# Seven products per pair: three of them take high and low token parts as one operand, and the order of the work around them

## What is computed

```python
def swiglu(x, w_gu, w_down):
    a, b = jnp.split(x @ w_gu, 2, axis=-1)
    return (jax.nn.silu(a) * b) @ w_down

for i in range(DEPTH):          # DEPTH = 2
    x = layer_norm(ALPHA * x + 0.5 * swiglu(x, ffn1_w_gu[i], ffn1_w_down[i]), ...)
    y, qm = gla_mix(x @ gla_w_in[j], ...)      # layer 0; conv_mix in layer 1
    m = mem_attention(qm, mem, mem_w_kv[i])
    x = layer_norm(ALPHA * x + jnp.concatenate([y, m], axis=-1) @ w_out, ...)
    x = layer_norm(ALPHA * x + 0.5 * swiglu(x, ffn2_w_gu[i], ffn2_w_down[i]), ...)
```

## Time and profile before

| | |
|---|---|
| median of three runs | 2028.52 us (2028.18 to 2030.37) |
| the profiled execution's own time | 2027.72 us |
| its span | 2025.7 us |
| granted clock of TensorE, mean | 0.998 |
| TensorE | 2007.7 us busy, 99% |
| VectorE | 1355.1 us, 67% |
| ScalarE | 811.9 us, 40% |
| GpSimd | 816.3 us, 40% |

### The profile page before, as it was taken

How to read it: one execution, slowest core, us unless ns; L and a number is a source line. 1 busy time by engine, 2 the same in 40 slices (tenths; PEclk the granted TensorE clock), 3 DMA queues, 4 the chain that set the end, 5 groups by cost and what they waited for, 6 DMA issues and landing times.

```text
span 2025.7 us, 33884 instructions
## 1 busy us (share of the span) xinstructions
PE 2007.7 (99%) x13253; PEld 1839.4 (91%) x13253; DVE 1355.1 (67%) x1851; ACT 811.9 (40%) x1165; POOL 816.3 (40%) x575
## 2 busy tenths in 40 slices
PE   9999999999999999999999999999999999999998
PEld 9899998888988999999899999989887799999887
DVE  4477774554425768887466888746899986777646
ACT  5433351263433354444234444423353434434422
POOL 1588830044423357880015877001100435887000
PEclk9999999999999999999999999999999999999999
DMA  7533332332212235453232545323544222332222
GB/s 253 208 125 124 124 130 91 113 102 67 84 32 73 96 103 164 147 166 107 92 103 94 166 145 166 107 95 101 187 125 177 83 97 92 104 104 93 86 96 99
DMA packets 227015, 239.10 MB, mean 118 GB/s; under 512 B 5935, under 2 KB 219309, under 8 KB 225132
## 3 DMA queue, kind: packets, MB, share of 16 engines
q1 hardware_dynamic: 225196, 234.63, 35.2%
q10 hardware_dynamic: 1728, 3.21, 0.5%
HBM read 215.80 MB, written 22.02 MB: 117 GB/s over the span
## 4 chain that ended last, share of the span: by engine, by line
PE 89%; DVE 4%; POOL 3%; ACT 2%; issue 2%; DMA 1%; DVEq 0%; SPq 0%; ACTq 0%; POOLq 0%
PE bank L1879 12%; PE bank L1881 12%; PE bank L1880 12%; PE bank L2015 11%; PE bank L2017 11%; PE bank L2016 11%; PE bank L1890 3%; PE bank L1891 3%; PE bank L1892 3%; PE bank L1969 1%; ACT whi L712 1%; DVE wlo L1191 1%; PE bank L1974 1%; PE bank L2339 1%; PE bank L2338 1%
## 5 line engine op out<-in xcount | busy, mean ns | idle before, releaser
L712 ACT CAST whi<-raw 128x2048 fp32r<-128x2048 f32 (+3 forms) x190 | 322.8, 1699 | 866.2 <-POOL scratch L596 435.0
L1191 DVE TENSOR_TENSOR wlo<-raw,whi 128x2048 fp32r<-128x2048 f32 (+2 forms) x164 | 360.9, 2200 | 232.9 <-ACT whi L712 232.7
L573 POOL TENSOR_TENSOR tiny<-tiny 128x2 f32<-128x2 f32 (+1 forms) x13 | 9.4, 726 | 567.1 <-DVE tiny L1471 567.1
L536 POOL TENSOR_TENSOR wlo<-raw,whi 128x256 fp32r<-128x256 f32 x128 | 101.5, 829 | 300.4 <-DVE wlo L1191 176.2
L592 POOL TENSOR_TENSOR raw<-raw 128x512 f32<-128x512 f32 x72 | 217.2, 3017 | 0.0
L1879 PE MATMUL bank<-h_hi,whi 128*128 128x512 f32 x528 | 207.1, 392 | 0.0
L1881 PE MATMUL bank<-h_hi,wlo 128*128 128x512 f32 x528 | 205.5, 389 | 0.0
L1880 PE MATMUL bank<-h_lo,whi 128*128 128x512 f32 x528 | 205.5, 389 | 0.0
L596 POOL TENSOR_TENSOR scratch<-raw,s 128x512 f32<-128x512 f32 x72 | 152.9, 2124 | 53.7 <-DVE ex_lo L1198 53.7
L2015 PE MATMUL bank<-t_hi,ex_hi 128*128 128x256 f32 x576 | 164.0, 285 | 1.5 <-DVE bank L1250 0.9
L2015 PE MATMUL bank<-t_hi,whi 128*128 128x256 f32 x576 | 163.7, 284 | 1.7 <-DVE bank L1258 1.7
(11 more groups left out here) (376 smaller groups left out, 5807.9 us busy)
## 6 DMA issues: line engine op xcount, KB each, us to landing
raw<-in_ffn_w_gu_dram SPq DMA_DIRECT2D x88, 1024.0 KB, 4.9
raw<-in_ffn_w_down_dram SPq DMA_DIRECT2D x32, 896.0 KB, 4.6
raw<-in_ffn_w_down_dram SPq DMA_DIRECT2D x32, 512.0 KB, 3.4
raw<-in_gla_w_in_dram SPq DMA_DIRECT2D x14, 1024.0 KB, 5.1
early_raw<-in_conv_w_in_dram SPq DMA_DIRECT2D x18, 512.0 KB, 4.2
lo_scratch<-early_lo SPq DMA_DIRECT2D x18, 512.0 KB, 3.3
diag_scratch<-diag_tmp SPq DMA_DIRECT2D x8, 1024.0 KB, 7.8
raw<-in_conv_w_in_dram SPq DMA_DIRECT2D x16, 512.0 KB, 5.1
```

The source lines that it names most:

```text
L536: last = nc.gpsimd.tensor_tensor(to[:, k, :], whole[:, k, :], high[:, k, :].bitcast(F32), ALU.subtract)
L712: nc.scalar.copy(whi[:, s, 0:kc, 0:width], raw[:, s, 0:kc, 0:width]).then_inc(hi_ready, 1)
L1191: nc.vector.tensor_tensor(wlo[:, s, 0:kc, 0:width], raw[:, s, 0:kc, 0:width], whi[:, s, 0:kc, 0:width].bitcast(F32), ALU.subtract).then_in ...
```

## The change

- `xhi` and `xlo` become two halves of one tensor `x_both`, `t_hi` and `t_lo` of `t_both`. Products 1, 2 and 4 of a group (`wide_product`) send high and low tokens through the high weights as one operand of 512 columns, and the high tokens through the low weights as 256, so 8 instructions for 12. The result of the low tokens lies in the other half of the bank.
- VectorE brings the halves together: step 0 copies the low half of product 1 and subtracts both; step 1 copies and adds; after step 3 the first result and `first_copy` are added. `first_copy` is the low half of products 1 and 4, copied by ScalarE (`first_rest`) after product 4.
- The four multiplications of a pair move behind the next pair's step 0 (`gated`).
- ScalarE's silu and VectorE's multiplications wait for the new addition too (`first_done`).
- In the output projections `residual_pair(ln, 1, ...)` comes before `split_lo(n0 + 6, 0)`, and TensorE does the memory parts of both pairs of blocks before the mixer's part of either.
- In the attention mixer `gates_of_r(0, 2)` moves into `keys_and_att(0)`, ahead of the products that wait for `pt_evac`.

```diff
-        xhi = sb("xhi", [P, DK, SEQ], F32R)
-        xlo = sb("xlo", [P, DK, SEQ], F32R)
+        x_both = sb("x_both", [P, 2, DK, SEQ], F32R)
+        xhi, xlo = x_both[:, 0, :, :], x_both[:, 1, :, :]
...
+            def first_rest(f, i, g):
+
+                act.wait_ge(first_done, summed(f, i, g) + 1)
+                act.wait_ge(first_mm, summed(f, i, g) + 1)
+                nc.scalar.copy(first_copy[:, :], bank[4 * g][:, HALF:SEQ]).then_inc(first_lo_out, 1)
...
                 if step == 0:
-                    nc.vector.tensor_scalar(r6, r1, -1.0, None, ALU.mult).then_inc(part_done, 1)
+                    nc.vector.tensor_copy(p5_copy[:, :], bank[b][:, HALF:SEQ]).then_inc(top_lo, 1)
+                    dve.wait_ge(top_lo, q + 1)
+                    nc.vector.scalar_tensor_tensor(out=r6, in0=r1, scalar=-1.0, in1=p5_copy[:, :], op0=ALU.mult,
+                                                   op1=ALU.subtract).then_inc(part_done, 1)
                 elif step == 1:
-                    nc.vector.tensor_copy(p5_copy[:, :], r5).then_inc(part_done, 1)
+                    dve.wait_ge(part_done, 4 * q + 1)
+                    nc.vector.tensor_copy(p5_copy[:, :], r5).then_inc(fifth_lo, 1)
+                    dve.wait_ge(fifth_lo, q + 1)
+                    nc.vector.tensor_tensor(p5_copy[:, :], bank[b + 1][:, 0:HALF], p5_copy[:, :], ALU.add).then_inc(part_done, 1)
...
                     nc.vector.tensor_tensor(r5, r6, p5_copy[:, :], ALU.add).then_inc(part_done, 1)
+                    dve.wait_ge(first_lo_out, q + 1)
+                    nc.vector.tensor_tensor(r1, r1, first_copy[:, :], ALU.add).then_inc(first_done, 1)
...
             def residual_out(ln, n0):
                 residual_pair(ln, 0, n0 + 3, 1.0, OUT_BANKS[0], scaled=(0,) if ln == LN_CONV_OUT else ())
+                residual_pair(ln, 1, n0 + 4, 1.0, OUT_BANKS[1])
                 split_lo(n0 + 6, 0)
-                residual_pair(ln, 1, n0 + 4, 1.0, OUT_BANKS[1])
...
+            def wide_product(b, w_hi, w_lo, both, start):
+
+                for k in range(4):
+                    nc.tensor.matmul(bank[b][:, :], w_hi[:, k], both[:, :, k], start=(start and k == 0), stop=False,
+                                     skip_group_check=True)
+                    last = nc.tensor.matmul(bank[b][:, 0:HALF], w_lo[:, k], both[:, 0, k], start=False, stop=(k == 3),
+                                            skip_group_check=True)
+                return last
...
-                product(r1, *weight(top, left), *x(top, early), True).then_inc(part_mm, 1)
+                wide_product(b, *weight(top, left), x_both[:, :, top, early], True).then_inc(part_mm, 1)
                 pe.wait_ge(ex_lo_ready, 2 * q + 2)
-                product(r5, *weight_sum(0), *x_sum(0), True).then_inc(part_mm, 1)
+                wide_product(b + 1, *weight_sum(0), t_both[:, :, 0, :, :], True).then_inc(part_mm, 1)
                 pe.wait_ge(part_done, 4 * q + 1)
                 product(r6, *weight_sum(1), *x_sum(2)).then_inc(part_mm, 1)
-                product(r1, *weight(low, left), *x(low, early))
+                wide_product(b, *weight(low, left), x_both[:, :, low, early], False).then_inc(first_mm, 1)
...
                         if h == 0:
-                            pe.wait_ge(lo_ready, n0 + 5 + p)
-                            pe.wait_ge(y_evac, Y_BASE[ln] + 2 * p + 2)
-                            memory_part(0)
-                            memory_part(1)
+                            for ahead in range(2 if p == 0 else 0):
+                                pe.wait_ge(lo_ready, n0 + 5 + ahead)
+                                pe.wait_ge(y_evac, Y_BASE[ln] + 2 * ahead + 2)
+                                memory_part(ahead, 0)
+                                memory_part(ahead, 1)
                             pe.wait_ge(lo_ready, n0 + 7 + p)
...
                 else:
+                    gates_of_r(0, 2)
                     pe.wait_ge(pt_evac, 2 * HEADS)
```

More of the change, by code:

```diff
@@ L53 @@
 OUT_K = 12
-ALIGN = 112
+ALIGN = 48
 ROW_G, ROW_B = 0, DEPTH * 3 * DK
@@ L322, in build @@
             sem(n) for n in ("w_sum", "ex_hi_ready", "ex_lo_ready", "part_mm", "part_done", "t_sum", "t_hi_ready", "t_ready"))
+        fifth_lo, top_lo, first_mm, first_lo_out, first_done = (
+            sem(n) for n in ("fifth_lo", "top_lo", "first_mm", "first_lo_out", "first_done"))
         conv_evac, glu_done, taps_done, conv_pad, tap_split, cin_hi_done, cin_done = (
@@ L740, in ffn_pair @@
                 if by_sums:
+                    act.wait_ge(first_done, summed(f, i, 0) + 2)
                     for n, b in enumerate((0, 3, 2, 1)):
@@ L1282, in summed_pair @@
                     extra_lo(f, i + 1, 0)
[L1283 to L1289 removed]
+                if last:
+                    gated(f, i)
             def blk(x, d):
@@ L1539, in ffn @@
                 dve.wait_ge(mul_done, gated_by(f, PLAIN))
-                with dve.Fori(PLAIN, FK // 2 - 1) as i:
+                summed_pair(f, PLAIN, first=True)
+                with dve.Fori(PLAIN + 1, FK // 2 - 1) as i:
                     summed_pair(f, i)
-                summed_pair(f, FK // 2 - 1)
+                summed_pair(f, FK // 2 - 1, last=True)
                 residual_ffn(f, LN_FFN[f], FFN_N[f] + FK)
@@ L1590, in mem_low @@
                                             ALU.subtract).then_inc(mem_ready, 1)
+            nc.vector.memset(first_copy[:, :], 0.0).then_inc(first_done, 1)
             mem_low(range(4))
```

43 lines of the change are left out of this document (26 added, 17 removed).

## The result

The changed kernel takes 2048.96 us (median of 5 runs, 2046.43 to 2053.39) where the kernel before takes 2028.18 (5 runs, 2027.02 to 2030.37). The ratio is 1.0104, 95% interval 1.0092 to 1.0116: 20.8 us slower. The prediction said 2046.5. The profiled execution of the changed kernel was the slowest of its five (2053.39, span 2051.7), so its trace shows 26.0 us over before's span of 2025.7, five more than the medians.

The account below looks back on a forecast made before the run. TensorE, busy 2007.7 of 2025.7 us, was taken as the bound. Stages +11.8, projections +7.5 and gates -1.0 sum to +18.3 on 2027.7, or 2046.0; beside the median 2046.8 it said 2046.5 us, range 2023 to 2056.

Parts of the forecast that it names:

- The stall and its growth: Stages two and three: second group's product 3 waits on step 0, about 0.8 us per pair, growing; +7.6 and +6.6 us.
- typical: Pair of the kernel before's second stage, 795.31 to 815.58, 20.27 us, from which the prediction counted its times.
- Rival B: Stages two and three: stall of 0.8 doesn't grow, split gets its turn ahead of L592; pairs 20.65, total 2037; chance 0.14.
- Rival D: Stages two and three: step 0 in time, early_lo takes 1.22; no slower than before, 2026.5 us; chance 0.11.
- The last stage: Fourth stage of seven products, without early_lo: step 0 never late, groups take about 10.04 after some three; 1.0 us gained.
- the ring: Last stage: load, sums and split of weight chunks form a loop of 10.05 to 10.1 us that holds back TensorE's groups.
- The gain on TensorE: Stages of seven products: wide products save 0.144 us per group, 10.4 us over 72 groups if nothing stands in the way.
- The first stage: First stage of seven products: 2.6 us gained less 1.2 of added stalls where GpSimd builds diagonals, 1.4 us gained.
- The projections: Two output projections: residual wait of 3.2 us and later GpSimd blocks delay the last quarter, +3.8 and +3.7 us.
- The gates: Attention mixer: gates moved ahead fill TensorE's 1.2 us wait on ScalarE, less 0.2 for a change of tile; -1.0 us.
- Moving the multiplications: VectorE, first group of a pair: the four multiplications behind step 0 end 0.5 before product 5, so moving them costs nothing.

Follow-up runs that it names:

- experiment 2: Changed kernel with early_lo's subtraction cut to 4 of 1024 elements per partition in all pairs but a stage's first: 2035.73 us, ratio 1.0032.
- experiment 4: Kernel before, products all of 256 columns, with one extra VectorE copy each in step 0 and step 1: 2047.36 us, ratio 1.0086.
- experiment 6: Changed kernel with early_lo's subtraction behind step 0 of the second group instead of ahead of it: 2033.78 us, ratio 1.0022.
- experiment 7: Changed kernel with GpSimd's first two sums cut to one block in four in the last stage, all pairs but its first: 2047.24 us (one run).
- experiment 11: Changed kernel with TensorE doing the first memory part twice in layer 0's output projection; total not in the text, last quarter 17.95 us after the first memory product.
- experiment 9: Kernel before with both edits of the output projections and nothing else: the edits cost 8.9 us by themselves.
- experiment 8: Wide products in stages one and four only, narrow with single operations in two and three, projections as before, gates as changed: 2026.91 us, 0.9992 of the kernel before.
- experiment 1: Changed kernel with both edits of the output projections undone: 2042.19 us, ratio 1.006.
- experiment 3: Kernel before with early_lo's subtraction cut to 4 of 1024 elements per partition in all pairs but a stage's first: 2027.86 us, ratio 0.9993.

## Why the prediction was right, point by point

**The stall and its growth** held: 16 waits on step 0, 15.1 us in all (15 to 20 forecast), early_lo at 2.31, the split behind L596; pairs of 21.4 for 21.37, stages two and three at 190.63 and 190.44 for 189.7. The waits themselves were a little shorter than I had worked out, 0.5 to 0.6 for 0.7 at first and 1.0 for 1.2 when grown. The pair of the kernel before that I called typical (20.27) is one of the slower ones: the last four pairs of its stage two take 20.16, with no stall. Experiments 2, 4 and 6 show the chain, not only its end: without early_lo, or with it one step later, both effects go; with VectorE's copies alone both come.

**Rival B** (no growth) hung on who asks first, the split or GpSimd's third sum; I had the split 0.1 us too late, and in the changed kernel it was 0.02 to 0.25 late in every pair. What its turn is worth shows where chance gave it. The kernels of experiments 7 and 11 have these stages as changed, and in three pairs with a wait of 1.0 the split got its turn and a pair with early_lo followed. One of them, of experiment 11, and the wait of product 3 in the next pair:

```profile
900.25 2.28 DVE L1206 TENSOR_TENSOR wlo<-raw,whi 128x2048 fp32r<-128x2048 f32 x1
...
900.25 3.42 POOL L596 TENSOR_TENSOR raw<-raw 128x512 f32<-128x512 f32 x1
...
919.35 0.39 PE L2048 MATMUL bank<-t_both,ex_hi 128*128 128x256 f32 x1 [0.56 <-DVE bank L1267]
```

In all three that wait is 0.55 or 0.56 instead of 1.0: the stall stays and its growth is gone, as rival B says. The pair doesn't gain all of it at once, since its first group then takes 10.3 to 10.5 (21.1 to 21.3 for the pair); in one place, in experiment 7, another such pair follows and takes 20.70, beside rival B's 20.65.

**Rival D** needed step 0 to start before 11.8 of its pair; it started at 13.1.

**The last stage** gave 0.9 for the forecast 1.0, and experiment 7 bears out the ring: it was met after eight groups, not after some three, since a group saves 0.09 and not 0.15.

**The gain on TensorE was mis-sized.** This is the term that was wrong in size. A wide product takes 1.41, not 1.39: 0.2325 us for a wide instruction (9.99 less 60 narrow ones of 0.120, over 12) in place of the 0.228 that I took from the stream of 512-column products. A group without a stall takes 9.99 (179.77 / 18), so 0.09 less than before and not 0.144, 6.5 us in all instead of 10.4. The rule of the Trainium skill that I weighed (TensorE: Matmul & The Clock Gate, "Back-to-back issue gap") would have given 2.2, as an estimate; the measurement lies between. In three stages it hardly moved the sum, since stalls or the ring swallow the difference; in the first it is most of the miss.

**The first stage** was forecast at -1.4 and gained about 0.2: seven kernels with wide products and their additions took 184.6 to 185.8 there (mean 185.2), five with plain narrow ones 185.2 to 185.9 (mean 185.4). Beside 179.8 for 18 groups without a stall the mean leaves 5.4 of stalls, and I had added 1.2 for less slack to 4.1, so 5.3. What was short is the gain, 1.6 instead of 2.6. (The one trace of the changed kernel, 185.79, is the slowest of the seven, with stalls of 6.0.) That GpSimd's diagonals set the time there, whatever TensorE saves, was argued and not tested.

**The projections** were forecast at +3.8 and +3.7 and cost +4.5 and +5.7 in this execution, +4.0 and +4.3 in experiment 9; seven kernels with both edits lie at 88.97 to 90.14 in layer 0 (91.23 with the fill) and 87.85 to 89.79 in layer 1. Counted from the first memory product (667.6 in the kernel before, 668.35 here), the residual is done after 6.8 us, not 6.1, and GpSimd's blocks after 18.0, not 17.4. VectorE's operations take what I reckoned, but between them it waits 0.79 for ScalarE, whose cast of the next chunk (669.96) stands ahead of the square that VectorE needs: so the wait on the residual is 3.94, not 3.2. In experiment 9 VectorE doesn't wait there, and its last quarter starts after 17.5. And I had nothing for TensorE's clock, which in layer 1 of the changed kernel falls after the second wait, on the path: 1.4.

**The gates** gained 1.5, not 1.0 (experiment 8): the whole wait of 1.25 is gone, and the 0.2 that I had put against it for a change of tile doesn't show. **Moving the multiplications** cost nothing (experiment 8), as said; that it gains in the first stage is likely from experiment 4's 0.9 and wasn't isolated.

So 20.8 us in the medians: 13 to 17 from early_lo and step 0 (experiments 2 and 6), 7 to 9 from the projections (1 and 9), and some 2.5 gained at the gates and in the first and last stage. The forecast of 18.3 isn't owed to errors that cancel: but for the gates, every term came out on the side of more loss, and that makes most of what the forecast lacks. Experiment 6 with the projections undone should by these numbers stand at 2025 to 2027, at or a little under the kernel before. It wasn't tried.

## What to carry to other kernels

Fewer instructions on the busiest engine bring little where the groups are already paced by a ring of others (here load, sums and split, groups of 10.03 to 10.19 us beside 9.99): write down each ring's length beside the engine's before costing the gain. Where two engines take turns at a resource, give for each operation of a group when it asks and who asked before it; here some hundredths of a microsecond decided whether a delay of 0.55 grew to 1.0 in the next iteration, and an operation that nobody waits for belongs behind the one that somebody waits for. If an engine's wait is filled with work, ask first what it will wait for next. And a gain of 1 us is read in a window of 10, not of 380.

## What the runs showed of the hardware

- The clock granted to TensorE fell to the lower level (0.50, 1.2 of 2.4 GHz) after waits of 3.94 and 6.6 us, but the length of the wait alone doesn't tell: it stayed at 1.00 after 1.83 us in the kernel before (layer 0), fell to 0.50 after the same 1.83 us of the same code in experiment 3, and was 0.66 over the three us after 1.75 us in experiment 11, where shorter waits of 0.78 and 0.39 had come just before.
- The same instructions at the same place run at 0.59 or at 1.00 in different executions (615 to 620 us), which makes up to 3 us between two traces of one code (375.9 and 379.0 from stage one to the projection, experiment 11 and the changed kernel). Terms below that can be read only in windows that leave such places out.
- A wide instruction of 512 columns whose two halves lie 16 KB apart took 0.2325 us among 256-column ones, against 0.228 in a stream of 512-column products and 0.240 for two narrow instructions. Whether the 0.005 comes from the halves or from the narrow instructions between was not tested.
- VectorE's split (both operands in SBUF) and GpSimd's sums take turns as whole instructions: 2.28 us alone, 3.19 to 3.43 where it asks 0.02 to 0.25 after L596, while VectorE's additions with operands in PSUM took 0.42 to 0.43 where they lay wholly inside such a sum (41 of L1279 inside L596).
